# A hybrid diffusion step: half of attention's exchange DMAs issued by GpSimd instead of ScalarE, modulation chunks in every second item, late chunks one per projected tile

## The reference

```python
mod = (jax.nn.silu(c) @ w_ada[l] + b_ada[l])[:, None, :]     # (1024) @ (1024, 6144), 24 MB a layer
sh1, sc1, g1, sh2, sc2, g2 = jnp.split(mod, 6, axis=-1)
h = rmsnorm(x, p['norm1_g']) * (1 + sc1) + sh1
...
s = jnp.einsum('bqhd,bkhd->bhqk', qi, k).astype(jnp.float32) * scale   # 4 heads
p = jax.nn.softmax(s, axis=-1).astype(v.dtype)
attn = jnp.einsum('bhqk,bkhd->bqhd', p, v)                    # latent: 1536 keys; prompt: 256
...
out = jnp.concatenate([attn_out, conv_out, cmlp_out], axis=-1) @ p['w_out']
x = x + g1 * out
h = rmsnorm(x, p['norm2_g']) * (1 + sc2) + sh2                # then the experts, x = x + g2 * ...
```

## Time and profile before

| | |
|---|---|
| Median of 3 runs | 2451.83 us (2449.34 to 2454.82) |
| The profiled execution | 2456.23 us, its span 2454.5 us |
| Mean granted clock of TensorE | 0.975 |
| TensorE busy | 2314.3 us (94%) |
| Its weight loads | 1517.4 us (62%) |
| VectorE busy | 744.8 us (30%) |
| ScalarE busy | 513.2 us (21%) |
| GpSimd busy | 279.4 us (11%) |
| SyncE's, GpSimd's, ScalarE's DMA queue | 46.5%, 9.4%, 4.9% of 16 engines' span |
| DRAM traffic | 158 GB/s over the span |

### The profile page before, as it was taken

One profiled execution on the slowest core, in us unless ns is written; L12 is line 12 of the kernel. 1 busy time (PEld: TensorE's weight loads), 2 busy tenths in 40 slices (PEclk: granted clock), 3 DMA queues, 4 the chain that ended last, 5 costly groups with the idle time before them and its releaser, 6 DMA issues.

```text
span 2454.5 us, 30238 instructions
## 1 busy us (share of the span) xinstructions
PE 2314.3 (94%) x12252; PEld 1517.4 (62%) x12252; DVE 744.8 (30%) x1409; ACT 513.2 (21%) x1050; POOL 279.4 (11%) x438
## 2 busy tenths in 40 slices
PE   6999997999799899999999999899999959999996
PEld 4545554555445787888765455456554448887885
DVE  2401244544236211111124012455523551111113
ACT  3310121222234211011033101222223320101003
POOL 2000011101000112111120000211100011112111
PEclk9999998999899999999999999999999979999998
DMA  9100279767425788888971002696642268888888
GB/s 333 35 4 18 66 161 216 163 136 138 180 95 190 272 271 282 276 271 270 346 247 35 7 15 68 141 203 122 134 126 95 86 229 274 272 275 280 275 278 298
DMA packets 216025, 440.70 MB, mean 180 GB/s; under 512 B 32033, under 2 KB 75225, under 8 KB 215937
## 3 DMA queue, kind: packets, MB, share of 16 engines
q1 hardware_dynamic: 169200, 360.28, 46.5%
q0 software_dynamic: 22928, 54.56, 9.4%
q10 hardware_dynamic: 23808, 24.66, 4.9%
HBM read 339.34 MB, written 47.65 MB: 158 GB/s over the span
## 4 chain that ended last, share of the span: by engine, by line
PE 84%; DMA 6%; DVE 4%; SPq 3%; ACT 1%; issue 1%; ACTq 1%; DVEq 0%; POOLq 0%
PE PS L1408 11%; PE PS L1415 11%; PE PS L1237 11%; PE PS L1440 9%; PE PS L1019 8%; PE PS L1169 6%; PE PS L973 6%; PE PS L1112 5%; PE PS L960 4%; DMA r<-r 4%; PE PS L1124 2%; PE PS L1434 2%; PE PS L1073 1%; PE PS L1393 1%; SPq L554 1%; DMA r<-in_x_sample_dram 1%
## 5 line engine op out<-in xcount | busy, mean ns | idle before, releaser
L1408 PEld LDWEIGHTS PS<-r,ring 128*128 128x128 f32 x2048 | 281.5, 190 | 16.0 <-issue 16.0
L1237 PE MATMUL PS<-ring,mix 128*128 128x512 f32 x640 | 289.0, 599 | 0.0
L1408 PE MATMUL PS<-r,ring 128*128 128x160 f32 x2048 | 283.6, 299 | 1.2 <-ACT r L1731 1.2
L1415 PE MATMUL PS<-r,ring 128*128 128x160 f32 x2048 | 283.4, 299 | 0.0
L1415 PEld LDWEIGHTS PS<-r,ring 128*128 128x128 f32 x2048 | 279.9, 190 | 0.0
L1440 PE MATMUL PS<-ring,r 128*128 128x512 f32 x496 | 221.2, 599 | 0.0
L1019 PE MATMUL PS<-r,ring 128*128 128x512 f32 (+1 forms) x576 | 208.4, 521 | 1.6 <-ACT r L1532 1.6
L1237 PEld LDWEIGHTS PS<-ring,mix 128*128 128x128 f32 x640 | 117.5, 191 | 128.8 <-issue 128.6
L1169 PE MATMUL PS<-r 128*128 128x256 f32 x768 | 176.6, 388 | 21.1 <-DMA r<-r 21.1
L1112 PE MATMUL PS<-lat,r 128*128 128x512 f32 (+1 forms) x416 | 188.7, 588 | 7.7 <-ACT ring L1594 5.1
L1169 PEld LDWEIGHTS PS<-r 128*128 128x128 f32 x768 | 149.0, 195 | 56.9 <-DMA r<-r 24.4
(11 more groups left out here) (304 smaller groups left out, 2184.9 us busy)
## 6 DMA issues: line engine op xcount, KB each, us to landing
ring<-in_w_gate_dram SPq DMA_DIRECT2D x32, 2048.0 KB, 10.1
ring<-in_w_up_dram SPq DMA_DIRECT2D x32, 2048.0 KB, 11.7
ring<-in_w_down_dram SPq DMA_DIRECT2D x31, 2048.0 KB, 9.4
ring<-in_w_ada_dram SPq DMA_DIRECT2D x15, 2048.0 KB, 9.8
r<-ring SPq DMA_DIRECT2D x144, 96.0 KB, 6.1
r<-r SPq DMA_DIRECT2D x128, 96.0 KB, 5.3
r<-r ACTq DMA_DIRECT2D x128, 96.0 KB, 5.5
r<-ring ACTq DMA_DIRECT2D x112, 96.0 KB, 5.8
```

Of the source, the lines that this page charges most:

```text
L1237: ins = pe.matmul(psum(2 * (s % 2) + n, 512), mix[:, k, tile * P:(tile + 1) * P], W_OUT[n][:, k, :], start=(k == 4), stop=(k == 3))
L1408: ins = pe.matmul(PS[:, b // 2, (b % 2) * 256:(b % 2) * 256 + SLOTS], W_G[:, k, b * P:(b + 1) * P], XST[par][:, k, :], start=(k == 0), sto ...
L1415: ins = pe.matmul(PS[:, 2 + b // 2, (b % 2) * 256:(b % 2) * 256 + SLOTS], W_U[:, k, b * P:(b + 1) * P], XST[par][:, k, :], start=(k == 0), ...
```

## The change

Three things change.

**Who issues the exchange.** Quarters 2 and 3 are issued by GpSimd, in all 18 items; quarters 0 and 1 by SyncE, also in the last. ScalarE issues none. GpSimd's eight stand ahead of `store_gate` and `spread_inverses` of the same item. They count on a semaphore of their own, `pt_pooled`, and each item's wait until those of the item before have landed. TensorE's values product and ScalarE's exponents now wait for both semaphores.

**Where chunks stand.** A table gives the item of each chunk: 0, 1, 3, 5, 7, 9, 11, 13 in layer 0 and 0, 1, 3, 5 in layer 1. The loads of chunks and of `w_out` follow: a chunk's load now stands ahead of the exchange of the item in which the chunk two before it is computed.

**The late chunks of the projection.** Of the three that went out ahead of the loop over tiles, one now goes out at each of tiles 2, 3 and 4, behind that tile's residual load.

```diff
@@ the tables
+CHUNK_ITEMS = [0, 1, 3, 5, 7, 9, 11, 13]
...
+def chunk_at(l, n):
+
+    return CHUNK_ITEMS.index(n) if n in CHUNK_ITEMS[:len(ADA_ITEMS[l])] else -1
@@ SyncE, attention
                 for n in range(NI):
-                    load_ada_weights(n + 2)
-                    exchange(n, (0, 1) if n < NI - 1 else range(4))
-                    load_ada_bias(n + 2)
-                    if n == len(ADA_ITEMS[l]):
+                    i = chunk_at(l, n)
+                    if i >= 0:
+                        load_ada_weights(i + 2)
+                    exchange(n, (0, 1))
+                    if i >= 0:
+                        load_ada_bias(i + 2)
+                    if i == len(ADA_ITEMS[l]) - 2:
                         sp.wait_ge(ada_summed, 1 + ADA_AT[l] + len(ADA_ITEMS[l]) - 1)
                         unit(2, (W_OUT[0], w_out_src[l, 0]))
-                    if n == len(ADA_ITEMS[l]) + 1:
+                    if i == len(ADA_ITEMS[l]) - 1:
                         sp.wait_ge(ada_summed, 1 + ADA_AT[l] + len(ADA_ITEMS[l]))
                         unit(0, (W_OUT[1], w_out_src[l, 1]))
@@ SyncE, projection
-                sp.wait_ge(pt_landed[0], at(l, 256 * NI // 2, 256 * NI // 2))
+                sp.wait_ge(pt_landed[0], at(l, 128 * NI // 2, 128 * NI // 2))
+                sp.wait_ge(pt_pooled, at(l, 128 * NI, 128 * (NI - 1)))
                 load_xd(0)
                 load_xd(1)
-                if l == 0:
-                    sp.wait_ge(uvh_summed, at(l, NU, NU))
-                    load_tail_chunk(0)
-                    load_tail_chunk(1)
-                    load_tail_chunk(4)
                 for t in range(NT):
...
                     if t + 2 < NT:
                         load_xd(t + 2)
+                    if l == 0 and 2 <= t <= 4:
+                        sp.wait_ge(uvh_summed, at(l, NU, NU))
+                        load_tail_chunk((0, 1, 4)[t - 2])
@@ GpSimd, attention
+                def exchange(n, quarters):
+
+                    groups, x = groups_of(n)
+                    pool.wait_ge(p_turned, at(l, 2 * NI, 2 * n + 2))
+                    if n >= 2:
+                        pool.wait_ge(o_summed, at(l, NI, n - 1))
+                    if n:
+                        pool.wait_ge(pt_pooled, at(l, 128 * NI, 128 * n))
+                    for a in quarters:
+                        for b in range(4):
...
+                            pool.dma_start(dst[:, :, x * b:x * (b + 1)], src[:, :, x * a:x * (a + 1)])\
+                                .then_inc(pt_pooled, 16)
...
                 for n in range(NI - 1):
-                    store_gate(n)
+                    exchange(n, (2, 3))
+                    store_gate(chunk_at(l, n))
                     spread_inverses(n)
+                exchange(NI - 1, (2, 3))
@@ TensorE, times_values
-                        pe.wait_ge(pt_landed[n % 2], at(l, 256 * NI // 2, 256 * (n // 2 + 1)))
+                        pe.wait_ge(pt_landed[n % 2], at(l, 128 * NI // 2, 128 * (n // 2 + 1)))
+                        pe.wait_ge(pt_pooled, at(l, 128 * NI, 128 * (n + 1)))
@@ TensorE, attention
-                    turn_modulation(n - 1)
+                    turn_modulation(chunk_at(l, n - 1))
...
-                    modulation(n)
+                    modulation(chunk_at(l, n))
@@ ScalarE, exponents
-                        act.wait_ge(pt_landed[n % 2], at(l, 256 * NI // 2, 256 * (n // 2)))
+                        act.wait_ge(pt_landed[n % 2], at(l, 128 * NI // 2, 128 * (n // 2)))
+                        act.wait_ge(pt_pooled, at(l, 128 * NI, 128 * (n - 1)))
@@ ScalarE, attention
-                def exchange(n, quarters):
...
-                    if n < NI - 1:
-                        exchange(n, (2, 3))
@@ VectorE, attention
-                    copy_modulation(n - 1)
+                    copy_modulation(chunk_at(l, n - 1))
...
-                    bias_modulation(n)
+                    bias_modulation(chunk_at(l, n))
```

More of the change, by code:

```diff
@@ L369, in backbone @@
         p_turned = sem("p_turned")
+        pt_pooled = sem("pt_pooled")
         pt_landed = [sem(f"pt_landed{i}") for i in range(2)]
@@ L738, in store_gate @@
                                     .then_inc(ada_stored[i % 2], 16)
+                def exchange(n, quarters):
[7 more added lines that the diff above has]
+                        for b in range(4):
+                            dst = turned(n)[32 * a:32 * a + 32, 0:4 * groups * x].rearrange("p (g x) -> p g x", g=groups)
+                            src = Pr[n % 2][32 * b:32 * b + 32, 0:4 * groups * x].rearrange("p (g x) -> p g x", g=groups)
+                            pool.dma_start(dst[:, :, x * b:x * (b + 1)], src[:, :, x * a:x * (a + 1)])\
+                                .then_inc(pt_pooled, 16)
                 def spread_inverses(n):
@@ L1620, in copy_value_heads @@
                     act.activation(mix[:, h, t0:t0 + 512], psum(bank, 512), ACT.Copy).then_inc(uvh_copied[0], 1)
-                def exchange(n, quarters):
-                    groups, x = groups_of(n)
-                    act.wait_ge(p_turned, at(l, 2 * NI, 2 * n + 2))
-                    if n >= 2:
-                        act.wait_ge(o_summed, at(l, NI, n - 1))
-                    for a in quarters:
-                        for b in range(4):
-                            dst = turned(n)[32 * a:32 * a + 32, 0:4 * groups * x].rearrange("p (g x) -> p g x", g=groups)
-                            src = Pr[n % 2][32 * b:32 * b + 32, 0:4 * groups * x].rearrange("p (g x) -> p g x", g=groups)
-                            act.dma_start(dst[:, :, x * b:x * (b + 1)], src[:, :, x * a:x * (a + 1)])\
-                                .then_inc(pt_landed[n % 2], 16)
                 for n in range(NI):
```

## The result

The changed kernel takes 2486.74 us (median of 4 runs, 2480.30 to 2491.14), the kernel before 2453.28 over its 4 runs: a ratio of 1.0156, 95% interval 1.0130 to 1.0182. It is 1.6% slower. The profiled execution took 2488.20 us, its span 2486.5, against 2456.23 and 2454.5.

A forecast was written before the change was run, and what follows sets the result against it. TensorE set the pace before; GpSimd's chain, 13.4 us an item against 13.3, would bind after. -15.4 + 4.5 + 18.6 + 4 = +11.7 on the median of 2451.8 gives 2463 us, range 2450 to 2500.

The forecast's parts named there:

- late chunks: Layer 0's projection: one load per tile removes the whole hole from waiting for the residual row, -15.4 us.
- layer 0's attention: Holes of 25 us close, but GpSimd's chain opens slightly more: +4.5 us.
- layer 1's: Attention of layer 1: GpSimd's chain delays the exchanges, 17.7 us by T(8), then 9 x 0.1: +18.6 us.
- the two tails: After each layer's attention, GpSimd's last exchange delays the gate-row loads and first add: 2 us per layer, +4.
- GpSimd's loop becomes the bound: Attention: GpSimd's chain takes 13.4 us per item against TensorE's 13.3, and 17.1 where it meets a load.
- Rivals 1 and 3: Attention: short issues and shallow load effect, 12.6 us per item, 2431 us, chance 0.25; GpSimd never binds, 2412, chance 0.07.
- The length of an item's loop: GpSimd per item: issues 4.8, reciprocal store 0.72, wait 7.3, spreading load 0.56, together 13.4 us.
- Which items meet a load: GpSimd's store waits 11.0 us in layer 0's items 2, 4, 6, 8, 10, 12 and layer 1's 2 and 4.
- rival 2: Attention: issues as forecast, but a load one item later hardly matters (wait 9.3 us); 2449 us, chance 0.14.
- The floor of the wait: GpSimd's wait for its reciprocal store to land is nearly a floor, taken as 7.3 us without a load.
- The spacing closes three holes: Layer 0's attention: chunks in every second item remove TensorE's three exchange waits, 25 us, if nothing else is late.
- ScalarE gives up eight issues, gain 0: Attention: taking eight exchange issues an item from ScalarE gains 0, since it idles between its exponents anyway.

The follow-up runs named there:

- the first four experiments: Late chunks alone (0.9912), exchange back on ScalarE (0.9969) and the move alone (1.0221), plus the changed kernel with its spreading load deferred (0.9863).
- the fastest: The changed kernel with GpSimd issuing each item's spreading load behind the next item's exchange: 0.9863 of the kernel before, 2416.32 us.

## Why the prediction was right, and which of its steps were not

The forecast was 2463 us, slower, by GpSimd's own loop. Measured were 2486.74, inside the range of 2450 to 2500. Direction and mechanism were right, but the loss is nearly three times the forecast's (33.5 us between the medians for 11.7), and slower had been given 0.46. Three of its terms were too small, and two of its reasons wrong. The terms, forecast and measured: late chunks -15.4 and -13.9, layer 0's attention +4.5 and +12.0, layer 1's +18.6 and +24.2, the two tails +4 and +10.5.

- **GpSimd's loop becomes the bound**: shown. It has hardly any idle time but the wait on its store, and its exchange of item 6 in layer 1 starts 105.2 us after T(0), where the text had 108. With the wait alone taken from between the exchanges, the loss goes. Rivals 1 and 3, in which GpSimd does not set the pace, are out with that. "Nearly every item" was too much: ScalarE's exponents wait for the exchange in 16 of the 32 latent items, and in layer 0's items 7, 9 and 11 it was SyncE's half that they waited for.
- **The length of an item's loop** is the term that was mis-sized. Eight exchange issues cost 4.3 us, not 4.8. The store's wait is 8.7 where no load runs, not 7.3. In the first six items of layer 1 the waits add up to 55.0 us, where the text has 55.9, so the cheaper issues bring T(8) early, 119.4 for a forecast of 123.3. After them the loop took 14.7 an item (exchanges 6 to 11), and the text counted "9 x 0.1": T(17) - T(8) is 130.7 instead of 121. Hence +24.2 for +18.6. In layer 0, with a mean wait of 9.9 over items 2 to 16, it is +12.0 for +4.5.
- **Which items meet a load**: wrong, and rival 2 comes in here. In items 2, 4, 6, 8, 10 and 12 of layer 0 the wait was 9.7 on average, where the forecast has 11.0 and rival 2 has 9.3; but items 5, 7, 9 and 11, counted at 7.3, had 11.0 to 12.5. Rival 2's total of 2449 fails on these and on the longer wait without a load.
- **The floor of the wait** was read from rows in which the store shared no queue with an exchange. Ahead of GpSimd's exchange it is nearly back (7.8). By the Trainium skill, page "DMA: Bandwidth & Descriptors", section "Anatomy of one DMA — SWDGE (gpsimd) path", the fixed part is about 2.0 us; the shortest of these waits was 7.1 in the changed kernel, so the trace disagrees, and ScalarE's queue was no shorter.
- **Late chunks, -15.4**: the hole closed, with 15.6 by itself and 13.9 in the changed kernel, where the second add came 1.7 later.
- **The tail, +4**: 8.8 and 1.7. The text had the last exchange start 12.0 after T(17); it started 16.8 after it in layer 0 and 14.4 in layer 1, which is the loop's length again.
- **The spacing closes three holes**: wrong. With ScalarE issuing, it closed none and cost 14 us; every second item still has its load ahead of its exchange, behind a wait for TensorE. With GpSimd issuing and the load deferred the holes are gone (2.0 us of waits), but there the spacing is worth 4 us at most, which is unclear. It is partly luck that the total came out inside the range: the holes that stayed are part of layer 0's +12.0, where the text has them closed and counts GpSimd's chain alone.
- **ScalarE gives up eight issues, gain 0**: not borne out with chunks spaced. With GpSimd's wait out of the way, half of the exchange on GpSimd is worth 0.9969 - 0.9863 = 1.1%, 26 us, against ScalarE issuing it. With one chunk an item it is 8 us and unclear. What makes the gain was not tested apart. Two rows bear on it: GpSimd's eight issues take 4.3 us, while one of ScalarE's takes 0.66 to 0.68 in the median, and a 96 KB DMA lands 4.2 to 5.0 us after GpSimd's issue in the changed kernel, against 5.5 to 5.8 after ScalarE's before (medians).

What stays open: in kernels where GpSimd's loop does not bind, layer 0's attention still differs by 40 us (231.6 to 271). The landing times put the longest on SyncE's half, late behind the chunk loads, and moving these loads took 31 us off layer 0; but one profile of each says little of the spread, and the kernel before took 2437.61 to 2461.07 us in the 17 runs beside the first four experiments. Nor is it known why the store's wait is longest, 10.7 us on average, with a quarter of the exchange on each of GpSimd and ScalarE.

## What to carry to other kernels

When work is given to an engine that looks idle, write down its loop for one round, waits included, and set it against the round of the engine that sets the pace: here 4.3 + 0.7 + 8.7 + 0.6 = 14.3 us against 13.3. Nothing urgent may stand behind an engine's wait for its own small store: issuing the dependent load one round later turned 1.6% lost into 1.4% won, 0.9 of which the late chunks give by themselves. And a load that waits for the slow engine to free its slot belongs ahead of an urgent transfer if it would otherwise arrive late itself (29 us lost behind it), and else behind it (17 us won). That rests on one pair each; in the changed kernel the load behind cost 12 us, and in the fastest it made no difference.

## What the runs showed of the hardware

- A store of 256 values of 4 bytes to DRAM keeps who waits for it 7.1 to 12.5 us in the changed kernel's latent items, issued by GpSimd, and 7.3 to 14.6 issued by ScalarE. The issue takes 0.72 and 0.37.
- GpSimd issues a DMA of 32 partitions by two runs in 0.53 us, hardly more than the 0.50 of a single run.
- Half of the exchange's 96 KB DMAs issued by GpSimd instead of ScalarE (the other half stays on SyncE, beside its 2 MB loads) took 26 us off a kernel with spaced chunks in which ScalarE had idle time for them, and 8 us, within the intervals, off one with a chunk an item.
- Behind a wait of 3.60 us TensorE's granted clock stood at 0.5 for 6.8 us, and a product of 5.34 us took 8.20.
